# Applying an RMS norm's factor to the results of the projections instead of to their input, in a fused three-layer kernel

## The chip, the cores and the metric

The kernel runs on one core of a Trainium2 chip. The metric is the device time of one launch in microseconds (us). Matrix products run on TensorE (PE in the profile; its weight loads are PEld), elementwise work on VectorE (DVE) and ScalarE (ACT); SyncE (SP) starts the loads of the weights.

## The reference

Three layers work on x, 256 tokens by 1024 features, in f32. The first two have this form (their feed-forward part is left out below, and so is the third layer, which the change does not touch):

```
h = rmsnorm(x, norm_mix[l])            # x * rsqrt(mean(x*x) + eps) * g
proj = h @ w_in[l]
aq, ak, av, iq, ik, iw, hq, hf, hi, hg, ga, gb = jnp.split(proj, split_points, axis=-1)
y_attn = dsa_attention(rope(norm(aq)), rope(norm(ak)), av, iq, ik, iw)   # top 64 keys per query
f = lb + (1 - lb) * sigmoid(hf)        # forget factor; the key is (1 - lb) * sigmoid(-hf)
o = recurrence(silu(hq), 1 - f, hi, f)
y_hgrn = rmsnorm(o) * silu(hg)
merged = sigmoid(ga) * (y_attn @ w_proj_attn[l]) + sigmoid(gb) * (y_hgrn @ w_proj_hgrn[l])
x = x + merged @ w_out[l]
```

The norm's factor, rsqrt(mean(x*x) + eps), is one number per token. So (x * factor * g) @ w equals factor * ((x * g) @ w).

## The kernel before

All weights come from HBM once, in units of 1 MB (half of that for some): `UNITS` lists them in the order in which PE uses them. A unit is loaded into one of six `raw` buffers. Then it is split into two parts of the type f32r: ACT writes `w_hi` (a rounded copy, `split` in the block of ScalarE, shown as L953), DVE writes `w_lo` (what is left, L1425). There are three buffers of each, so the split of unit m waits for the end of unit m-3 on PE. The activations are split in the same way, and each product is three matmuls: hi with hi, lo with hi, and hi with lo (`three`, L508 to L510).

Each of PE, ACT and DVE has its own stream of instructions in a fixed order, written out by hand, and passes it from the front. Semaphores tie the streams together. On ACT and DVE a call of `tick()` steps to the next unit and issues the split of the unit three ahead of it. `unit_in()` waits for PE to end a unit, `emptied()` frees its PSUM bank. There are four banks called `stream` for the units and four called `steps` for the rest.

In a mixer (the part of a layer ahead of its feed-forward part) the units are, in order: ix0, ix1 (index queries and keys), aq0, aq1, ak0, ak1, av0, av1 (attention), hf0, hf1 (forget), hq0, hq1, hg0, hg1 (recurrence), ga0, ga1 (gate), hi0, hi1, ga2, ga3, gb0 to gb3. Those with two banks (ix, aq, ak, av, hi) have tokens on the partitions; the others have features on the partitions, and their result is 128x512 for a unit, the two halves of the features side by side.

The norm is used in two ways. Up to ak1, PE multiplies the input times the norm's weights only (`x_gained_hi`, `x_gained_lo`), since the factor isn't known yet; ACT applies the factor when it empties the banks, as the scale of its copy. From av0 on PE multiplies the normalised input (`h_hi`, `h_lo`). `normalise` (L1492) makes it: DVE multiplies x, weight and factor into `h_norm` (8 instructions, L1506), ACT rounds it into `h_hi` (`normed_hi`, 4), DVE subtracts into `h_lo` (4, L1501).

Around the first of the two blocks of 128 queries, the streams are these. PE: hf1, then the first logits (L696), then hq0, then the transposes of the probabilities (L704), then hq1. DVE: the mask and the row maximum of each head from the logits (L1617, L1621), one split, the second half of the selection of keys for the second query block (`next(chosen[1])`, L1595 to L1604), two splits, then the keys and forget factors (L1798 to L1801), which wait for hf1. ACT: sigmoids of hf0 and hf1 straight from their banks (`scratch` and `hgrn_k_in_order`, L1206 and L1207), then the exponentials of the first block, one per head (`probs`, L1052), which wait for the row maximum.

```
1787  first, second = attend(b, 0, sel[:, 0, 0:P]), attend(b, 1, sel[:, 1, :])
1788  dve.wait_ge(*s_sel.at(b, 0))
1789  next(first)
1790  tick()
1791  next(chosen[1])
1792  tick(2)
1793
1794  dve.wait_ge(*evacuated(unit(b, "hf1")))
```

The second query block follows in the same way: logits after hg1, the transposes after ga0. ACT's exponentials of it come after its Silu of hg1.

Of the kernel before, what the change touches and what calls it, by code (L numbers as in the profile page):

```python
# [131 lines left out]
def scaled_after(u):  # L132
    return u[1] < 2 and (u[2] in ("ix0", "ix1", "aq0", "aq1", "ak0", "ak1") or u[0] in ("gate", "up") and u[2] < 2)
# [10 lines left out]
def evac_engine(u):  # L144
# [4 lines left out]
    if kind == "merge" or (kind == "out" and b < 2) or (kind == "gate" and scaled_after(u)) or name in ("val0", "val1", "f") or shifted(u):  # L149
        return "dve"  # L150
# [35 lines left out]
def build(nc, a, out):  # L186
# [26 lines left out]
    flip = at("reversed_ident", [P, P], F32, 155)  # L213
    v_back = at("v_reversed", [P, 512], F32, 173)
# [181 lines left out]
    g_sig = Event("gates_set", 2)  # L396
# [106 lines left out]
    def _(pe):  # L503
# [33 lines left out]
        def stream(count, before=None, between=None):  # L537

            for _ in range(count):
# [15 lines left out]
                h_h, h_l = (xg_h, xg_l) if scaled_after(UNITS[m]) else (xs_h, xs_l) if shifted(UNITS[m]) else (hh, hl)  # L555
# [109 lines left out]
        def normed(ni, pairs=range(4)):  # L665
            return {2 * j: [n_lo.at(ni, j)] for j in pairs}
# [119 lines left out]
        def mixer(b):  # L786
# [30 lines left out]
            stream(1, normed(ni, (0, 1)))  # L817
            stream(1, normed(ni, (2, 3)))
            stream(1)
# [24 lines left out]
            pe.wait_ge(*evacuated(unit(b, "hq1")))  # L844
# [98 lines left out]
    def _(act):  # L943
# [33 lines left out]
        def here():  # L977
            return cur[0] - 1
# [32 lines left out]
        def gained_hi(ni, g, j):  # L1011

            dst = xg_h if ni < 4 else xs_h[:, :, 0:T]
# [7 lines left out]
        def normed_hi(ni):  # L1021
            for j in range(4):
                act.wait_ge(*n_hn.at(ni, j))
# [95 lines left out]
        def mixer(b, x_ready):  # L1119
# [34 lines left out]
            for j in range(2):  # L1154
# [4 lines left out]
                else:  # L1159
# [3 lines left out]
                    normed_hi(2 * b)  # L1163
# [5 lines left out]
            act.wait_ge(*n_lo.upto(2 * b))  # L1169
# [28 lines left out]
            for j in range(2):  # L1198
                tick()
                unit_in()  # L1200
# [10 lines left out]
            unit_in()  # L1211
            f(hq[:, 0:2, :], b2(here()), ACT.Silu).then_inc(*emptied())
            next(first)
            tick()
            unit_in()
            f(hq[:, 2:4, :], b2(here()), ACT.Silu).then_inc(*emptied())
            tick()
            unit_in()
            f(hg[:, 0:2, :], b2(here()), ACT.Silu).then_inc(*emptied())
            next(first)  # L1220
            tick()
# [191 lines left out]
    def _(dve):  # L1413
# [328 lines left out]
        def mixer(b):  # L1742
# [80 lines left out]
            for i in range(7):  # L1823
# [6 lines left out]
                if i % 2:  # L1830
                    tick()
# [309 lines left out]
```

## Time and profile before

| what | value |
|---|---|
| median of 3 runs | 1191.14 us (1190.63 to 1192.18) |
| the profiled execution, its own time | 1191.75 us |
| its span in the trace | 1190.0 us |
| busy PE, DVE, ACT | 1138.2, 858.1, 631.4 us |
| mean granted clock of PE, as a share of full speed | 0.992 |

The profile shows one execution. The span runs from the first to the last instruction in the trace, and the time measured for the same execution is 1.75 us more. Times inside the trace count from the start of the span. In the trace the first mixer stands between about 11 and 230 us, the second between about 431 and 643 us. An instruction's row gives its start and its length; a group's row gives its total and mean, and in brackets how long its engine stood idle before it and what ended that.

### The profile page before, as it was taken

How to read it: one execution, taken by the hardware profiler on the slowest of the kernel's cores; microseconds unless marked ns; L12 is line 12 of the kernel's file. 1: busy time of each engine (PE TensorE's matmuls, PEld its weight loads, DVE VectorE, ACT ScalarE, POOL GpSimd, SP SyncE). 2: the span in 40 equal slices, each digit the busy share in tenths (PEclk: the TensorE clock that was granted, in tenths of full speed). 3: DMA queues.
4: the chain of work that ended last, by engine and by line, in shares of the span. 5: the costliest groups of instructions: out<-in, count | busy, mean ns of one | idle time of the engine just before them, and what ended most of it. 6: DMA issues, size and time to landing. Idle time of an engine off the chain costs nothing.

```text
span 1190.0 us, 20981 instructions
## 1 busy us (share of the span) xinstructions
PE 1138.2 (96%) x8858; PEld 1102.4 (93%) x8858; DVE 858.1 (72%) x1376; ACT 631.4 (53%) x790; POOL 0.2 (0%) x4
## 2 busy tenths in 40 slices
PE   5999999999999999999999999999999989999996
PEld 5789899999999998998999999999989879999996
DVE  6996566777988879956667778887899756554443
ACT  7676366464443456764655544444687555433333
POOL 0000000000000000000000000000000000000000
PEclk9999999999999999999999999999999999999998
DMA  9555433756879554464437488795443333655511
GB/s 347 155 175 177 142 116 133 235 191 225 278 251 318 173 171 152 144 186 131 142 128 254 150 270 277 250 305 161 136 161 123 106 106 107 208 182 177 177 36 36
DMA packets 177613, 214.14 MB, mean 180 GB/s; under 512 B 3696, under 2 KB 160752, under 8 KB 177520
## 3 DMA queue, kind: packets, MB, share of 16 engines
q1 hardware_dynamic: 176800, 211.86, 54.5%
q8 instruction: 70, 1.15, 0.4%
q10 hardware_dynamic: 720, 0.94, 0.2%
q14 instruction: 23, 0.19, 0.1%
HBM read 211.74 MB, written 1.05 MB: 179 GB/s over the span
## 4 chain that ended last, share of the span: by engine, by line
PE 72%; DVE 18%; ACT 7%; issue 2%; DMA 1%; SPq 0%; DVEq 0%; ACTq 0%
PE stream L508 16%; PE stream L510 16%; PE stream L509 16%; DVE w_lo L1425 7%; PE steps L508 5%; PE steps L510 5%; PE steps L509 5%; ACT w_hi L953 3%; PE steps L714 1%; PE stream L735 1%; PE steps L864 1%; DVE conv_acc L1995 1%; DVE h_norm L1506 1%; DVE score L1597 1%; ACT probs L953 1%
## 5 line engine op out<-in xcount | busy, mean ns | idle before, releaser
L1425 DVE TENSOR_TENSOR w_lo<-raw,w_hi 128x2048 fp32r<-128x2048 f32 (+2 forms) x178 | 401.2, 2265 | 207.2 <-ACT w_hi L953 206.6
L953 ACT ACTIVATE w_hi<-raw 128x2048 fp32r<-128x2048 f32 (+2 forms) x178 | 336.3, 1893 | 287.9 <-PE stream L510 256.9
L508 PE MATMUL stream<-h_hi,w_hi 128*128 128x256 f32 x1576 | 451.2, 286 | 8.4 <-DVE w_lo L1425 7.4
L509 PE MATMUL stream<-h_lo,w_hi 128*128 128x256 f32 x1576 | 445.8, 283 | 0.0
L510 PE MATMUL stream<-h_hi,w_lo 128*128 128x256 f32 x1576 | 445.8, 283 | 0.0
L508 PEld LDWEIGHTS stream<-h_hi,w_hi 128*128 128x128 f32 x1576 | 302.2, 192 | 13.1 <-DVE w_lo L1425 10.8
L509 PEld LDWEIGHTS stream<-h_lo,w_hi 128*128 128x128 f32 x1576 | 302.4, 192 | 1.0 <-issue 1.0
L510 PEld LDWEIGHTS stream<-h_hi,w_lo 128*128 128x128 f32 x1576 | 302.2, 192 | 0.0
L508 PE MATMUL steps<-gu_hi,w_hi 128*128 128x256 f32 x528 | 149.8, 284 | 1.5 <-DVE gu_lo L1727 1.5
L509 PE MATMUL steps<-gu_lo,w_hi 128*128 128x256 f32 x528 | 149.4, 283 | 0.0
L510 PE MATMUL steps<-gu_hi,w_lo 128*128 128x256 f32 x528 | 149.4, 283 | 0.0
L508 PEld LDWEIGHTS steps<-gu_hi,w_hi 128*128 128x128 f32 x528 | 101.3, 192 | 2.1 <-issue 1.8
L509 PEld LDWEIGHTS steps<-gu_lo,w_hi 128*128 128x128 f32 x528 | 101.3, 192 | 0.0
L510 PEld LDWEIGHTS steps<-gu_hi,w_lo 128*128 128x128 f32 x528 | 101.3, 192 | 0.0
L1681 DVE SCALAR_TENSOR_TENSOR ada_sum<-ada_raw,c_act,ada_sum 128x256 f32<-128x256 f32 x168 | 81.5, 485 | 6.0
L953 ACT ACTIVATE gu_hi<-gu 128x512 fp32r<-128x512 f32 x33 | 20.8, 632 | 102.8 <-DVE gu L1723 98.7
L581 PE MATMUL stream<-w_hi,x_gained_hi 128*128 128x512 f32 (+1 forms) x96 | 37.3, 388 | 11.4 <-DVE w_lo L1425 11.4
L1995 DVE SCALAR_TENSOR_TENSOR conv_acc<-conv_in,params,conv_acc 128x256 f32<-128x256 f32 x90 | 38.9, 480 | 1.0
L1727 DVE TENSOR_TENSOR gu_lo<-gu,gu_hi 128x512 fp32r<-128x512 f32 x33 | 22.9, 693 | 23.0 <-ACT gu_hi L953 23.0
L508 PE MATMUL stream<-x_gained_hi,w_hi 128*128 128x256 f32 x128 | 36.8, 287 | 1.0 <-DVE x_gained_lo L1479 1.0
L509 PE MATMUL stream<-x_gained_lo,w_hi 128*128 128x256 f32 x128 | 36.2, 283 | 0.0
L510 PE MATMUL stream<-x_gained_hi,w_lo 128*128 128x256 f32 x128 | 36.2, 283 | 0.0
(307 smaller groups left out, 1634.9 us busy)
## 6 DMA issues: line engine op xcount, KB each, us to landing
raw<-in_w_ffn_in SPq DMA_DIRECT2D x66, 1024.0 KB, 5.5
raw<-in_w_in SPq DMA_DIRECT2D x54, 1024.0 KB, 5.4
raw<-in_w_ffn_out SPq DMA_DIRECT2D x33, 1024.0 KB, 5.3
ada_raw<-in_ada_w SPq DMA_DIRECT2D x24, 1024.0 KB, 6.6
raw<-in_w_out SPq DMA_DIRECT2D x8, 1024.0 KB, 5.1
raw<-in_w_proj_attn SPq DMA_DIRECT2D x8, 512.0 KB, 3.5
raw<-in_w_proj_hgrn SPq DMA_DIRECT2D x8, 512.0 KB, 4.6
raw<-in_w_o SPq DMA_DIRECT2D x4, 1024.0 KB, 5.2
```

Source lines behind the costliest of these rows:

```text
L508: pe.matmul(dst, w_h, x_h, start=start, stop=False, skip_group_check=True)
L509: pe.matmul(dst, w_h, x_l, start=False, stop=False, skip_group_check=True)
L510: return pe.matmul(dst, w_l, x_h, start=False, stop=stop, skip_group_check=True)
L581: pe.matmul(dst, h_h[:, k0 + k, ts], hi[:, k, :], start=k0 + k == 0, stop=False)
L714: mm = pe.matmul(pv[:, DH * h:DH * h + DH], prT[:, h, s, :], v[:, s, DH * h:DH * h + DH], start=s == 0, stop=s == qt)
L735: mm = pe.matmul(conv_bank[:, 0:T], diag[j], upad[:, 3, j:j + T], start=j == 0, stop=j == CONV_K - 1)
L864: mm = pe.matmul(level_bank(i)[:, c, :], kp[i % 2][:, c, :], qp[:, c, :].rearrange("p (n two h) -> p n two h", two=2, h=h)[:, :, 1, :], st ...
L953: return act.activation(out_, in_, func, **kw)
L1425: tt(wl[m % SPL][:, 0:n], raw[m % RAW][:, 0:n], wh[m % SPL][:, 0:n].bitcast(F32), ALU.subtract)\
L1681: ins = stt(acc, w[:, k, :], cact[:, k:k + 1], acc, ALU.mult, ALU.add)
L1727: tt(gu_l[i % 2].rearrange("p c t -> p (c t)"), gu, gu_h[i % 2].rearrange("p c t -> p (c t)").bitcast(F32), ALU.subtract).then_inc(*lane.m ...
L1995: ins = stt(cv[:, c, :], src, w, cv[:, c, :], ALU.mult, ALU.add)
```

## The change

In the first two layers PE multiplies the input times the norm's weights in every unit of the mixer. It is now held in `h_hi` and `h_lo` (ACT and DVE write it there where they wrote `x_gained`), and `normalise` is not called for these mixers. The factor is applied to results:

- hf, hq, hg, ga0, ga1, gb2 and gb3 (10 units per mixer) are emptied by DVE, which multiplies the bank by the factor (`scaled_evac`, into `scratch`, `hgrn_q`, `hgrn_gate`, `gate_a`, `gate_b`). The sigmoids and Silus of ACT then read these tiles and wait for DVE.
- ga2, ga3, gb0 and gb1 are still copied by ACT, and DVE multiplies them in place later, four features' chunks at a time.
- av and hi get the factor as a scale of ACT's copy.
- The factor is copied to `rstd_kept`, since `gate_b` covers the tile `rstd`.

The diff, cut to its core:

```diff
 def scaled_after(u):
-    return u[1] < 2 and (u[2] in ("ix0", "ix1", "aq0", "aq1", "ak0", "ak1") or u[0] in ("gate", "up") and u[2] < 2)
+    return u[1] < 2 and (u[0] in ("tw", "fm") or u[0] in ("gate", "up") and u[2] < 2)
+def scaled_by_dve(u):
+    return u[1] < 2 and u[2] in ("hf0", "hf1", "hq0", "hq1", "hg0", "hg1", "ga0", "ga1", "gb2", "gb3")
...
# TensorE, mixer
-            stream(1, normed(ni, (0, 1)))
-            stream(1, normed(ni, (2, 3)))
-            stream(1)
+            stream(3)
...
# ScalarE, mixer
-                    normed_hi(2 * b)
...
-            act.wait_ge(*n_lo.upto(2 * b))
...
-                unit_in()
                 for i in range(2 * (1 - j)):
                     act.wait_ge(*qk_t.at(b, 2 + i))
...
-                act.wait_ge(*s_used.at(b, 1))
-                f(scr[:, 2 * j:2 * j + 2, :], b2(here()), ACT.Sigmoid).then_inc(*lane.step())
-                f(hkn[:, 2 * j:2 * j + 2, :], b2(here()), ACT.Sigmoid, scale=-1.0).then_inc(*emptied())
+                act.wait_ge(*evacuated(here()))
+                z = scr[:, 2 * j:2 * j + 2, :]
+                f(hkn[:, 2 * j:2 * j + 2, :], z, ACT.Sigmoid, scale=-1.0).then_inc(*lane.step())
+                act.wait_ge(*lane.last)
+                f(z, z, ACT.Sigmoid).then_inc(*lane.mark(f_act))
             first, second = attend(b, 0), attend(b, 1)
+            def activated(x, event):
+                tick()
+                act.wait_ge(*evacuated(here()))
+                f(x, x, ACT.Silu).then_inc(*lane.mark(event))
             next(first)
+            activated(hq[:, 0:2, :], q_act)
+            next(first)
+            activated(hq[:, 2:4, :], q_act)
+            activated(hg[:, 0:2, :], hg_act)
+            next(first)
+            activated(hg[:, 2:4, :], hg_act)
+            next(second)
...
# VectorE, mixer
-            normalise(2 * b, lambda k: pc("norm_mix", 8 * b + k))
...
+            def scaled_tick(dst):
+                step()
+                scaled_evac(dst)
+                split_ahead()
             next(first)
-            tick()
+            scaled_tick(scr[:, 0:2, :])
             next(chosen[1])
-            tick(2)
-            dve.wait_ge(*evacuated(unit(b, "hf1")))
+            scaled_tick(scr[:, 2:4, :])
+            scaled_tick(hq[:, 0:2, :])
+            dve.wait_ge(*f_act.at(b, 1))
...
+            dve.tensor_copy(rs_kept, rs).then_inc(*lane.step())
+            scaled_tick(hq[:, 2:4, :])
             next(first)
-            tick()
+            scaled_tick(hg[:, 0:2, :])
             next(first)
             dve.wait_ge(*s_sel.at(b, 1))
             next(second)
-            tick(3)
+            scaled_tick(hg[:, 2:4, :])
+            scaled_tick(ga[:, 0:2, :])
+            scaled_tick(ga[:, 2:4, :])
             next(second)
...
+            wide_rs = rs_kept.unsqueeze(1).broadcast_to([P, 4, T])
+            dve.wait_ge(*evacuated(unit(b, "ga3")))
+            tt(ga[:, 4:8, :], ga[:, 4:8, :], wide_rs, ALU.mult).then_inc(*lane.mark(g_scaled))
             tick()
-            tick()
+            dve.wait_ge(*evacuated(unit(b, "gb1")))
+            tt(gb[:, 0:4, :], gb[:, 0:4, :], wide_rs, ALU.mult).then_inc(*lane.mark(g_scaled))
+            scaled_tick(gb[:, 4:6, :])
...
-            tick()
+            step()
+            scaled_evac(gb[:, 6:8, :], rs_kept)
+            split_ahead()
```

How the instructions stand, first on VectorE in the first mixer, from the row maximum of the first query block to the split after the selection of keys (rows that repeat are left out). Before:

```order
L1621 SCALAR_TENSOR_TENSOR row_max<-row_max,qk_sumsq 128x8
L1425 TENSOR_TENSOR w_lo_60<-raw_54,w_hi_57 128x2048
L1595 MAX top_188<-score 128x8
L1597 MATCH_REPLACE score<-top_188,score 128x256
...
L1602 TENSOR_SCALAR sel_bias<-score 128x256
L1604 SCALAR_TENSOR_TENSOR sel_bias<-sel_bias,consts 128x256
L1425 TENSOR_TENSOR w_lo_58<-raw_49,w_hi_55 128x2048
```

Now (the two reads of `stream` are hf0 and hf1):

```order
L1620 SCALAR_TENSOR_TENSOR row_max<-row_max,qk_sumsq 128x8
L1488 TENSOR_TENSOR scratch<-stream,rstd 128x512
L1424 TENSOR_TENSOR w_lo_60<-raw_54,w_hi_57 128x2048
L1594 MAX top_189<-score 128x8
L1596 MATCH_REPLACE score<-top_189,score 128x256
...
L1601 TENSOR_SCALAR sel_bias<-score 128x256
L1603 SCALAR_TENSOR_TENSOR sel_bias<-sel_bias,consts 128x256
L1488 TENSOR_TENSOR scratch<-stream,rstd 128x512
L1424 TENSOR_TENSOR w_lo_58<-raw_49,w_hi_55 128x2048
L1488 TENSOR_TENSOR hgrn_q<-stream,rstd 128x512
```

Hf0 is emptied behind the row maximum, hf1 behind the selection. On ScalarE at the same place, from the copies of the keys to the exponentials of the first query block, the order of instructions is the same, but the inputs are others. Before:

```order
L953 ACTIVATE kT<-steps 128x512 x2
L953 ACT_TABLE_LOAD
L953 ACTIVATE scratch<-stream 128x512
L953 ACTIVATE hgrn_k_in_order<-stream 128x512
L953 ACTIVATE w_hi_55<-raw_49 128x2048
L953 ACTIVATE scratch<-stream 128x512
L953 ACTIVATE hgrn_k_in_order<-stream 128x512
L953 ACT_TABLE_LOAD
L953 ACTIVATE probs,row_sum<-probs,row_max,qk_sumsq 128x128 x8
```

Now:

```order
L960 ACTIVATE kT<-steps 128x512 x2
L960 ACT_TABLE_LOAD
L960 ACTIVATE hgrn_k_in_order<-scratch 128x512
L960 ACTIVATE scratch<-scratch 128x512
L960 ACTIVATE w_hi_55<-raw_49 128x2048
L960 ACTIVATE hgrn_k_in_order<-scratch 128x512
L960 ACTIVATE scratch<-scratch 128x512
L960 ACT_TABLE_LOAD
L960 ACTIVATE probs,row_sum<-probs,row_max,qk_sumsq 128x128 x8
```

The sigmoids ahead of `probs` now read what DVE has written to `scratch`. The third place is VectorE at the second query block, from its row maximum on (hg1, ga0 and ga1). Now:

```order
L1620 SCALAR_TENSOR_TENSOR row_max<-row_max,qk_sumsq 128x8
L1488 TENSOR_TENSOR hgrn_gate<-stream,rstd 128x512
L1424 TENSOR_TENSOR w_lo_59<-raw_53,w_hi_56 128x2048
L1488 TENSOR_TENSOR gate_a<-stream,rstd 128x512
L1424 TENSOR_TENSOR w_lo_60<-raw_54,w_hi_57 128x2048
```

Before, the three splits stood there alone; the multiplications of `hgrn_gate` and `gate_a` are new.

## Rows read from the trace of the kernel before

**Rows 1.** The page: busy us, share of the span, instructions of each engine.

```profile
PE 1138.2 (96%) x8858; PEld 1102.4 (93%) x8858; DVE 858.1 (72%) x1376; ACT 631.4 (53%) x790; POOL 0.2 (0%) x4
```

**Rows 2.** PE's waits from 0 to 215 us: us in total, times, longest us.

```profile
PE stream L508 <- DVE w_lo L1425: 2.3, 2, 1.2
PE steps L675 <- DVE q_tm L1566: 1.3, 1, 1.3
...
PE steps L675 <- DVE k_tm L1574: 0.2, 1, 0.2
```

**Rows 3.** PE's waits from 430 to 630 us, the second mixer.

```profile
PE stream L508 <- DVE w_lo L1425: 1.9, 2, 1.2
```

**Rows 4.** PE's waits over the whole span.

```profile
PE steps L887 <- ACT scratch L953: 0.8, 2, 0.4
```

**Rows 5.** A stretch: length, busy PE, PEld, DVE, ACT, POOL, granted clock, DMA.

```profile
60.00:70.00 10.00, 9.76 (x67) 8.79 (x67) 9.72 (x14) 5.92 (x8) 0.00 (x0) 1.00 0.61 194
```

**Rows 6.** Groups by line and shape: count, busy us, mean ns, idle before.

```profile
L1506 DVE SCALAR_TENSOR_TENSOR h_norm<-xT,params,rstd 128x256 f32<-128x256 f32 x32 | 13.7, 479 | 0.0
L1501 DVE TENSOR_TENSOR h_lo<-h_norm,h_hi 128x512 fp32r<-128x512 f32 x16 | 11.0, 687 | 0.7 <-ACT h_hi L953 0.3
L1489 DVE TENSOR_TENSOR silu_g<-stream,rstd 128x512 f32<-128x512 f32 x4 | 2.7, 684 | 0.0
L953 ACT ACTIVATE silu_g<-silu_g 128x512 f32<-128x512 f32 x4 | 2.5, 632 | 5.9 <-DVE silu_g L1489 5.9
```

**Rows 7.** Instructions of DVE, first query block, first mixer: start us, us.

```profile
80.15 0.28 DVE L1617 CUSTOM_DVE_ANT_0 probs<-steps,sel_bias 128x128 f32<-128x128 f32 x1
...
81.96 0.17 DVE L1621 SCALAR_TENSOR_TENSOR row_max<-row_max,qk_sumsq 128x8 f32<-128x8 f32 x1
82.04 2.29 DVE L1425 TENSOR_TENSOR w_lo<-raw,w_hi 128x2048 fp32r<-128x2048 f32 x1
84.25 0.42 DVE L1595 MAX8 top<-score 128x8 f32<-128x256 f32 x1
...
88.84 2.29 DVE L1425 TENSOR_TENSOR w_lo<-raw,w_hi 128x2048 fp32r<-128x2048 f32 x1
```

**Rows 8.** Instructions of ACT, the same place.

```profile
80.27 0.59 ACT L953 ACTIVATE hgrn_k_in_order<-stream 128x512 f32<-128x512 f32 x1
80.88 1.28 ACT L953 ACT_TABLE_LOAD   x1
82.17 0.50 ACT L953 ACTIVATE probs<-probs,row_max,qk_sumsq 128x128 f32<-128x128 f32 x1
...
85.93 0.19 ACT L953 ACTIVATION_READ_ACCUMULATOR probs<-probs,row_max,qk_sumsq 128x1 f32 x1
```

**Rows 9.** Instructions of PE, the same place: logits, hq0's first, transposes.

```profile
77.81 1.26 PE L696 MATMUL steps<-kT,qT 64*128 64x128 f32 x16
80.29 0.39 PE L508 MATMUL stream<-h_hi,w_hi 128*128 128x256 f32 x1 [1.22 <-DVE w_lo L1425]
...
86.17 0.55 PE L704 MATMUL steps<-consts,probs 128*128 128x128 f32 x3
```

**Rows 10.** ACT, second mixer: the square of the attention queries.

```profile
456.98 1.06 ACT L953 ACTIVATE qk_square<-q_tm 128x1024 f32<-128x1024 f32 x1
```

**Rows 11.** DVE, second mixer: its next step, which reads that square.

```profile
459.04 1.21 DVE L1563 TENSOR_REDUCE qk_sumsq<-qk_square 128x16 f32<-128x1024 f32 x1
```

**Rows 12.** Second query block, first mixer, ACT and PE.

```profile
111.06 0.60 ACT L953 ACTIVATE probs<-probs,row_max,qk_sumsq 128x256 f32<-128x256 f32 x1 [0.52 <-DVE row_max L1621]
...
115.91 1.31 PE L704 MATMUL steps<-consts,probs 128*128 128x128 f32 x10 [1.18 <-ACT probs L953]
```

**Rows 13.** Stretches at PE's wait in the third layer (columns as in 5).

```profile
974.00:979.37 5.37, 0.00 (x0) 0.03 (x1) 4.13 (x10) 3.33 (x9) 0.00 (x0) 0.72 0.40 159
979.37:983.30 3.93, 3.93 (x17) 3.72 (x17) 3.83 (x9) 1.96 (x5) 0.00 (x0) 0.52 0.00 0
983.30:985.59 2.29, 2.29 (x18) 2.19 (x17) 1.67 (x4) 2.26 (x4) 0.00 (x0) 1.00 0.04 11
```

More of the change, by code:

```diff
@@ L148, in evac_engine @@
         return "gu"
-    if kind == "merge" or (kind == "out" and b < 2) or (kind == "gate" and scaled_after(u)) or name in ("val0", "val1", "f") or shifted(u):
+    if scaled_by_dve(u) or kind == "merge" or (kind == "out" and b < 2) or (kind == "gate" and scaled_after(u)) or name in ("val0", "val1", "f") or shifted(u):
         return "dve"
@@ L554, in stream @@
                 before = None
-                h_h, h_l = (xg_h, xg_l) if scaled_after(UNITS[m]) else (xs_h, xs_l) if shifted(UNITS[m]) else (hh, hl)
+                h_h, h_l = (xg_h, xg_l) if scaled_after(UNITS[m]) and kind in ("gate", "up") else (xs_h, xs_l) if shifted(UNITS[m]) else (hh, hl)
                 def in_order(n_out, n_in):
@@ L665, in normed @@
         def normed(ni, pairs=range(4)):
-            return {2 * j: [n_lo.at(ni, j)] for j in pairs}
+            return {2 * j: [n_lo.at(NTH_NORM[ni], j)] for j in pairs}
         def gained(ni, pairs=range(4)):
@@ L843, in mixer @@
             pe.wait_ge(*r_k.at(b))
-            pe.wait_ge(*evacuated(unit(b, "hq1")))
+            pe.wait_ge(*q_act.at(b, 1))
             pe.wait_ge(*a_lo.at(b, 1))
@@ L1204, in mixer @@
                         .then_inc(*lane.mark(qkT_set))
[L1205 to L1207 removed]
+                act.wait_ge(*evacuated(here()))
[3 more added lines that the diff above has]
+                f(z, z, ACT.Sigmoid).then_inc(*lane.mark(f_act))
             first, second = attend(b, 0), attend(b, 1)
+            def activated(x, event):
+                tick()
+                act.wait_ge(*evacuated(here()))
+                f(x, x, ACT.Silu).then_inc(*lane.mark(event))
             next(first)
+            activated(hq[:, 0:2, :], q_act)
[5 more added lines that the diff above has]
+            next(second)
             tick()
[L1211 to L1213 removed]
+            next(second)
             tick()
[L1215 to L1233 removed]
             def pack(i):
@@ L1248, in mixer @@
             wide_evac(v)
-            gates = [ga[:, 2 * j:2 * j + 2, :] for j in (2, 3)] + [gb[:, 2 * j:2 * j + 2, :] for j in range(4)]
+            gates = [ga[:, 2 * j:2 * j + 2, :] for j in (2, 3)] + [gb[:, 2 * j:2 * j + 2, :] for j in range(2)]
             def copied(i, rows, t, n):
@@ L1282, in mixer @@
                     f(AT[:, :, 2, :], level_bank(i), ACT.Copy).then_inc(*lane.mark(r_copy))
-            act.wait_ge(*evacuated(unit(b, "ga3")))
+            act.wait_ge(*g_scaled.at(b, 0))
             f(ga, ga, ACT.Sigmoid).then_inc(*lane.mark(g_sig))
-            evac_copy(gates.pop(0))
+            tick()
             for i in range(2):
@@ L1807, in mixer @@
             next(second)
-            tick(3)
+            scaled_tick(hg[:, 2:4, :])
+            scaled_tick(ga[:, 0:2, :])
+            scaled_tick(ga[:, 2:4, :])
             next(second)
             tick()
-            dve.wait_ge(*evacuated(unit(b, "hq1")))
+            dve.wait_ge(*q_act.at(b, 1))
             for g in range(2):
```

36 lines of the change are left out of this document (14 added, 22 removed).

## The prediction

> **What bounds the kernel now.** I read the page's busy times first: PE is busy 1138.2 us of a span of 1190.0 [rows 1]. The change leaves PE's matmuls as they are. So the time can move only by PE's waits, and by the clock at which PE runs behind them. The table of PE's waits comes next. In the first mixer, 2.3 us go to splits that DVE delivered late, and 1.3 and 0.2 us to rotated queries and keys, also from DVE [rows 2]; in the second mixer, 1.9 us go to splits [rows 3]. These are the waits in which normalising can have a part: DVE is busy 9.72 us of 10 in such a stretch, while the clock is at its full level [rows 5]. Last I read where each engine stands around the first query block [rows 7 to 9], since the order of instructions shows that the change puts DVE between PE and ACT there.
>
> **What is taken away.** Per mixer DVE loses 8 multiplications at 0.48 us and 4 subtractions at 0.69 [rows 6]. Their sum is 6.6 us; as neighbours overlap by some 0.07 us, 5.8 remain. ACT loses four copies. DVE, which is full there, comes that much earlier to the late splits and rotations. In the first mixer all three kinds of wait are shorter than 5.8 us and go: -3.8 us. In the second, DVE's lead is smaller. Its first reduction of queries starts at 459.04 [rows 11] and needs ACT's square, done at 456.98 + 1.06 = 458.04 [rows 10]: at least 1.0 us of lead. The square itself comes earlier by at most the four copies that go, 4 x 0.63 = 2.5 us [rows 6]; most of these ran while ACT would have waited for PE. So the lead is 1.0 to 3.5 us, and I take 1.8, nearer to the end that has a row; that is about enough for both late splits: -1.9 us. PE's wait for the squares of the recurrence's output, 0.8 us over both mixers [rows 4], goes too, since ACT no longer copies gb2 ahead of them. Together -6.5 us.
>
> **What comes in at the first query block.** On ACT the exponentials stand behind the sigmoids of hf1, as before, but these now read what DVE has emptied, and DVE empties hf1 behind the selection of keys. From the end of the row maximum (82.13) the chain is now:
>
> - DVE empties hf0, 0.6 us (0.68 less the overlap) [rows 6], and makes its split, 84.25 - 82.04 = 2.2 us [rows 7];
> - the second half of the selection, 88.84 - 84.25 = 4.6 us [rows 7], and hf1 emptied, 0.7: so far 8.0 us from the row maximum, as the first step starts 0.1 before its end;
> - ACT's two sigmoids at 0.63 us [rows 6], the table load for the exponential, 1.3 us, which was hidden before, and the exponentials, 82.17 to 86.12, or 4.0 us with the passing on [rows 8].
>
> That makes 14.6 us, where it was 4.0. PE meanwhile has only hq0 to do, 86.17 - 80.29 = 5.9 us [rows 9]. The row maximum ended 82.13 - 79.07 = 3.1 us behind the logits; the masks and maxima alone take 2.0 us (80.15 to 82.13) and can start when the first pair of logits is out, some 0.8 us before the last (1.26 us for four pairs [rows 9], and a little to pass it on). So it ends 1.2 us behind them at best. In the first mixer, where DVE has its full lead, I take this: PE waits 1.2 + 14.6 - 5.9 = 9.9 us. In the second, the logits come 0.7 us earlier and DVE 1.8 us: the masks then start 1.1 - 1.1 = 0 us behind the logits, and PE waits 2.0 + 14.6 - 5.9 = 10.7 us. Sum +20.6 us; with 1.0 and 3.1 us at the ends, 19.4 to 23.6.
>
> What queues behind: PE's values, its later units and every split behind hq0 slide by the same amount, so that this wait isn't met again. The splits for hq1 and hg0 are ready before PE resumes.
>
> **The second query block.** DVE empties hg1 only behind the row maximum of this block, and ACT's Silu of hg1 stands ahead of its exponentials. Before, these started at once behind the row maximum (111.06, after a wait of 0.52), and PE waited 1.18 us [rows 12]. Now 0.6 us for the emptying, 0.63 for the Silu and 1.28 for the table load, which can't start before, come in between: +2.5 us, twice, +5.1.
>
> **The clock.** The wait of 5.37 us in the third layer shows what a long idle does. The mean granted clock over it is 0.72, then 0.52 for 3.93 us of matmuls, the level of 1.2 GHz. The same pieces of work take 2.29 us when it is back at 1.00 [rows 13]. That is 1.6 us lost, and each wait of 10 us must lose it too: +3.3 us. The second waits will be 3.7 us long, between 1.18 us, where nothing shows, and 5.37; so between 0 and 1.6 us each. They lie nearly in the middle, and I take 0.8: +1.6. The Trainium skill (TensorE: Matmul & The Clock Gate, HAM oscillation — how this bites in real kernels) says that an idle PE falls back to half clock and that half of the time spent there is lost; by that the 3.93 us would cost 2.0 instead of 1.6 us, and the sum would be 0.7 us higher.
>
> **The rest costs nothing.** Of the other emptyings, hq0 falls into DVE's time before PE resumes; hq1, hg0, ga0, ga1 come just behind the end of their unit, where DVE has to wait for ACT's half of the next split anyway. If that cover is gone, a split is 0.6 us later, and two units are still split ahead. The multiplications of ga2 to gb1, two of 128x1024, fall into idle time of DVE behind the recurrence; of gb2 and gb3 one replaces a copy of ACT. The scales on ACT's copies add little, on an engine with room (5.92 us of 10 [rows 5]). No queue of SP is touched; loads follow the splits.
>
> **Sum.** -6.5 + 20.6 + 5.1 + 3.3 + 1.6 = 24.1 us. The profiled execution took 1191.75 us (span 1190.0), 0.6 above the median of 1191.14, so I put the same sum on the median: 1215.2 us.
>
> **The rivals.**
> 1. *The clock costs nothing.* PE resumes with transposes and is soon level again. Against it speaks [rows 13]. It would give 24.1 - 4.9 = 19.2 us: 1210.3. Chance 0.10.
> 2. *A change of table costs more than its load.* Four loads that were hidden stand on the path. The trace shows no more than the load: it starts 0.02 us behind the sigmoid's end (80.27 + 0.59), and the exponential starts 0.01 us behind the load's end [rows 8]. A further 1.4 us at each of the four would give 1220.7 us. The Trainium skill (ScalarE: Activation LUTs, What ACT_TABLE_LOAD costs) gives 2.66 us for a switch, 1.38 of them a drain beside the load; the trace doesn't agree. Chance 0.05.
> 3. *DVE is the bound and the hold is short.* If the sigmoids of hf1 found DVE's result early, only DVE's added work would count: 10 emptyings at 0.6, two wide products of 1.2 each and a copy make 8.6 us against 5.8 taken away, +2.8 per mixer, or 5.6, with the second block's 5.1 and nothing gained: 1201.8. Against it: the order of instructions has the selection ahead of hf1. Chance 0.10.
> 4. *Faster: the hold is hidden.* The 6.5 us of waits go, and the exponentials still reach PE within its stream of hq0. Row maximum at 1.2 us and 4.0 us of exponentials leave 0.7 us of room against 5.9. The hold must then be under 0.7 us instead of 10.6, and the second block hidden too: 1184.6. With 5.1 us paid there, the kernel breaks even where the first hold is 1.4 us. Chance 0.04.
>
> That the change doesn't do what it says is ruled out by the order of the instructions, but an unforeseen cancellation stays: 0.02 for no change.
>
> **The numbers.** Forecast 0.69, rivals 0.10, 0.05, 0.10, 0.04, no change 0.02. Predicted 1215.2. The range holds forecast and rivals 1 and 2. Its low end takes no clock loss and the shortest waits (1210.3 - 1.2 = 1209.1), its high end the longest waits of the first block (+3.0) and 1.6 us for each clock loss (+1.6), 1219.8, and rival 2: 1208 to 1221. A measurement of this kernel can tell 0.2% or 2.4 us from no change. Slower by more 0.94, within 0.02, faster 0.04.
>
> **What would show it.** In the profile after: a wait of PE for `probs` of 9 to 12 us in each mixer, and one of 3 to 4 us, where each had 1.2; DVE's emptying of hf1 directly behind the selection; ACT's first exponential 9 to 11 us behind the row maximum; a granted clock near 0.5 behind the long waits; no wait for `q_tm` or `k_tm` and hardly one for `w_lo` in the mixers. I am wrong if PE's waits for `probs` sum to less than 15 us, or if the time falls.

## The result, and the profile after

The changed kernel is slower: 1223.57 us, the median of four runs (1222.69 to 1224.76), against 1191.46 us for the kernel before in four runs. The ratio is 1.027, with a 95% interval of 1.0255 to 1.0286. The profiled execution took 1223.65 us, with a span of 1221.5 us and a mean granted clock of 0.980. Against the profiled execution of before that is 31.9 us more, 31.5 of it in the span. The forecast was 1215.2 us with a range from 1208 to 1221: the direction was right and so were the places that it named, but one place was missing, and the time lies 2.6 us above the range.

The page of the profile after, busy times [rows 1] and clock:

```profile
PE 1144.9 (94%) x8858; PEld 1110.2 (91%) x8858; DVE 865.4 (71%) x1378; ACT 624.6 (51%) x774; POOL 0.2 (0%) x4
...
PEclk9999999999999999989999999999999998999998
```

PE has the same 8858 matmuls and is busy 6.7 us longer; its mean granted clock is 0.980, where it was 0.992. DVE gained 7.3 us, ACT lost 6.8; neither is near its limit. PE's waits over the whole span, after (us in total, times, longest):

```profile
PE steps L713 <- ACT probs L960: 28.3, 4, 10.4
PE stream L517 <- DVE gate_b L1488: 4.2, 2, 2.1
PE stream L517 <- DVE w_lo L1424: 4.2, 6, 1.2
```

The first row is the forecast one: four waits for `probs` in the mixers. The second was not forecast. No wait for `q_tm`, `k_tm` or the squares is left [rows 2, 4].

The first query block on DVE, which answers to [rows 7] (start us, us, engine, line, instruction, idle before it):

```profile
76.85 0.17 DVE L1620 SCALAR_TENSOR_TENSOR row_max<-row_max,qk_sumsq 128x8 f32<-128x8 f32 x1
76.93 0.68 DVE L1488 TENSOR_TENSOR scratch<-stream,rstd 128x512 f32<-128x512 f32 x1
77.53 2.28 DVE L1424 TENSOR_TENSOR w_lo<-raw,w_hi 128x2048 fp32r<-128x2048 f32 x1
...
83.99 0.43 DVE L1603 SCALAR_TENSOR_TENSOR sel_bias<-sel_bias,consts 128x256 f32<-128x256 f32 x1
84.33 0.68 DVE L1488 TENSOR_TENSOR scratch<-stream,rstd 128x512 f32<-128x512 f32 x1
```

The same place on ACT, as in [rows 8]:

```profile
78.32 0.63 ACT L960 ACTIVATE scratch<-scratch 128x512 f32<-128x512 f32 x1
78.86 1.90 ACT L960 ACTIVATE w_hi<-raw 128x2048 fp32r<-128x2048 f32 x1
85.05 0.63 ACT L960 ACTIVATE hgrn_k_in_order<-scratch 128x512 f32<-128x512 f32 x1 [4.29 <-DVE scratch L1488]
85.71 0.63 ACT L960 ACTIVATE scratch<-scratch 128x512 f32<-128x512 f32 x1
86.36 1.28 ACT L960 ACT_TABLE_LOAD   x1
87.66 0.49 ACT L960 ACTIVATE probs<-probs,row_max,qk_sumsq 128x128 f32<-128x128 f32 x1
```

And on PE, as in [rows 9]:

```profile
73.42 1.26 PE L705 MATMUL steps<-kT,qT 64*128 64x128 f32 x16
75.19 0.39 PE L517 MATMUL stream<-h_hi,w_hi 128*128 128x256 f32 x1 [0.50 <-DVE w_lo L1424]
...
91.63 1.97 PE L713 MATMUL steps<-consts,probs 128*128 128x128 f32 x8 [10.43 <-ACT probs L960]
```

One reads the hold from top to bottom: the row maximum ends at 77.02, hf0 is emptied, a split is made, the selection runs to its end, and only then hf1 is emptied (84.33). ACT stood idle 4.29 us for that. From the row maximum to PE's first transpose it is 91.63 - 77.02 = 14.6 us, to the tenth the number of the forecast.

What the trace says of the term that was missed, PE first, then DVE, at the start of the first mixer's merge units:

```profile
203.23 0.28 PE L519 MATMUL stream<-ya_hi,w_lo 128*128 128x256 f32 x1
205.60 0.36 PE L517 MATMUL stream<-ya_hi,w_hi 128*128 128x256 f32 x1 [2.09 <-DVE gate_b L1488]
...
206.15 0.42 PE L517 MATMUL stream<-ya_hi,w_hi 128*128 128x256 f32 x1
206.36 0.41 PE L518 MATMUL stream<-ya_lo,w_hi 128*128 128x256 f32 x1
```

```profile
198.58 1.23 DVE L1853 TENSOR_TENSOR scratch<-scratch,hgrn_gate 128x1024 f32<-128x1024 f32 x1
203.62 1.23 DVE L1855 TENSOR_TENSOR yh_lo<-scratch,yh_hi 128x1024 fp32r<-128x1024 f32 x1 [3.82 <-ACT yh_hi L960]
204.77 0.68 DVE L1488 TENSOR_TENSOR gate_b<-stream,rstd_kept 128x512 f32<-128x512 f32 x1
```

The second merge unit writes to the bank that holds gb3. Before, ACT copied gb3 out of it ahead of `yh_hi`, and PE came for the bank 0.2 us after the end of that copy. The rows of the kernel before, ACT, then PE:

```profile
191.26 0.57 ACT L953 ACTIVATE gate_b<-stream 128x512 f32<-128x512 f32 x1
191.73 1.05 ACT L953 ACTIVATE yh_hi<-scratch 128x1024 fp32r<-128x1024 f32 x1
...
192.06 0.28 PE L508 MATMUL stream<-ya_hi,w_hi 128*128 128x256 f32 x1
```

Now the step is DVE's and stands behind `yh_lo`, behind a wait of 3.82 us, so PE stops for 2.09 us. The matmuls behind that stop follow each other at 0.21 us (206.15 to 206.36); those ahead of it at 0.12. The granted clock was 1.00 over the stop and 0.50 from 206.15 to 209.10.

**The ledger.** Since PE's instructions are the same and in the same order, its loss can be read off as the shift of each piece of work. Starts on PE, us:

| piece of PE's work | before | after | shift | change of the shift |
|---|---|---|---|---|
| hq0, first mixer | 80.29 | 75.19 | -5.10 | -5.10 |
| transposes, first block | 86.17 | 91.63 | +5.46 | +10.56 wait |
| values, first block | 92.86 | 100.56 | +7.70 | +2.24 clock |
| transposes, second block | 115.91 | 126.14 | +10.23 | +2.53 wait |
| values, second block | 123.47 | 135.25 | +11.78 | +1.55 clock |
| squares of the recurrence | 181.61 | 192.90 | +11.29 | -0.49 |
| squares for the next norm | 242.10 | 257.19 | +15.09 | +3.80 gb3 |
| hq0, second mixer | 493.20 | 506.36 | +13.16 | -1.93 |
| transposes, first block | 499.07 | 522.81 | +23.74 | +10.58 wait |
| values, first block | 505.76 | 531.28 | +25.52 | +1.78 clock |
| transposes, second block | 528.80 | 556.86 | +28.06 | +2.54 wait |
| values, second block | 536.37 | 566.03 | +29.66 | +1.60 clock |
| squares of the recurrence | 594.51 | 623.68 | +29.17 | -0.49 |
| squares for the next norm | 655.00 | 686.47 | +31.47 | +2.30 gb3 |
| end of PE's work | 1179.86 | 1211.38 | +31.52 | +0.05 |

Sums: -8.0 gone, +26.2 in waits for the exponentials, +7.2 of clock behind them, +6.1 at gb3 (4.6 of wait in both mixers and 1.5 of clock in the first). The same reading is used for every experiment below. It compares single executions, and up to hq0 it carries some chance: ten profiles (the changed kernel's and those of its variants below) run the same instructions up to there, and hq0 starts in them between 75.13 and 76.38 us. The clock's share was read from stretches around the first wait (columns as in [rows 5]):

```profile
81.20:91.63 10.43, 0.00 (x1) 0.00 (x0) 6.41 (x13) 6.52 (x20) 0.00 (x0) 0.75 0.60 195
91.63:95.60 3.97, 3.97 (x19) 3.97 (x20) 2.19 (x1) 3.94 (x4) 0.00 (x0) 0.50 0.03 10
95.60:99.60 4.00, 4.00 (x31) 4.00 (x31) 2.80 (x8) 0.69 (x2) 0.00 (x0) 0.87 0.69 206
```

### The profile page after: what moved, and what is told of

It is laid out like the page before. It is cut to its first block, busy times and chain, and to the rows that moved or that the text cites. A ratio compares the mean times of both kernels' runs of the same rounds, so it can differ in the third digit from the quotient of the medians.

```text
span 1221.5 us, 20961 instructions
## 1 busy us (share of the span) xinstructions
PE 1144.9 (94%) x8858; PEld 1110.2 (91%) x8858; DVE 865.4 (71%) x1378; ACT 624.6 (51%) x774; POOL 0.2 (0%) x4
## 4 chain that ended last, share of the span: by engine, by line
PE 72%; DVE 16%; ACT 7%; issue 2%; DMA 1%; SPq 0%; DVEq 0%; ACTq 0%
PE stream L517 15%; PE stream L518 15%; PE stream L519 15%; DVE w_lo L1424 6%; PE steps L517 5%; PE steps L519 5%; PE steps L518 5%; ACT w_hi L960 3%; ACT probs L960 1%; PE steps L723 1%; DVE score L1596 1%; PE stream L744 1%; PE steps L871 1%; DMA raw<-in_w_in 1%; PE steps L713 1%
## 5 line engine op out<-in xcount | busy, mean ns | idle before, releaser
L590 PE MATMUL stream<-w_hi,h_hi 128*128 128x512 f32 (+1 forms) x160 | 62.2, 388 | 12.1 <-DVE w_lo L1424 12.1
L592 PE MATMUL stream<-w_lo,h_hi 128*128 128x512 f32 (+1 forms) x160 | 60.5, 378 | 0.0
L591 PE MATMUL stream<-w_hi,h_lo 128*128 128x512 f32 (+1 forms) x160 | 60.4, 378 | 0.0
L590 PEld LDWEIGHTS stream<-w_hi,h_hi 128*128 128x128 f32 x160 | 30.7, 192 | 17.7 <-issue 12.1
```

Source lines behind the costliest of these rows:

```text
L590: pe.matmul(dst, h_h[:, k0 + k, ts], hi[:, k, :], start=k0 + k == 0, stop=False)
L591: pe.matmul(dst, h_l[:, k0 + k, ts], hi[:, k, :], start=False, stop=False)
L592: mm = pe.matmul(dst, h_h[:, k0 + k, ts], lo[:, k, :], start=False, stop=k0 + k == KC - 1)
```

## The experiments

**Theory A**: everything lost is PE's waiting for three results that stand late in their engine's order (hf1 behind the selection, hg1's Silu ahead of the second exponentials, gb3 behind `yh_lo`), and the lower clock behind these waits. Taking away the normalised input is itself worth 8 us. **The rivals**: the waits come from DVE's added work; gb3's wait only covers another; the low clock has nothing to do with the waiting; the change lost time in a further place. The kernel before ran beside each group of experiments, with medians of 1191.87 us (1 to 4), 1191.77 (5 to 8), 1191.35 (9, 10) and 1191.57 (11); "less" below is against the changed kernel's 1223.57.

### 1. gb3 emptied ahead of the wait

```diff
             tt(scr, scr, hg, ALU.mult).then_inc(*lane.mark(r_y))
+            step()
+            scaled_evac(gb[:, 6:8, :], rs_kept)
             dve.wait_ge(*r_hi.at(b))
             tt(yh_l, scr, yh_h.bitcast(F32), ALU.subtract).then_inc(*lane.mark(r_lo))
-            step()
-            scaled_evac(gb[:, 6:8, :], rs_kept)
             split_ahead()
```

> The changed kernel (1223.6 us) with one step of VectorE moved: it empties gb3 before it waits for the rounded yh, not behind yh_lo. Theory A (TensorE's 2.1-us wait for gb3's bank, ahead of the second merge unit of each mixer, is time of the kernel): both waits go, 4.2 us, and with the first mixer's wait the low granted clock behind it, up to 1.5 us: 1218 to 1219.5. Theory B (the wait only takes the place of one that comes next, for yh_lo or for the gates' sigmoids): under 1 us is won, 1222.6 to 1223.6, and a new wait of about 2 us stands at the same place under another name.

Measured: 1216.63 us, 6.9 less than the changed kernel and 1.4 below A's range. PE's wait for `gate_b` is gone and no other has come; DVE has the step within its old idle time:

```profile
201.11 0.69 DVE L1488 TENSOR_TENSOR gate_b<-stream,rstd_kept 128x512 f32<-128x512 f32 x1 [0.86 <-PE stream L519]
```

In the ledger the two pieces up to the next norm's squares shrink by 3.79 and 2.29 us, the 3.80 and 2.30 of the table. The other 0.8 us is in places that the edit doesn't touch: this profile reached hq0 1.06 us later, lost 0.72 and 0.30 us less of clock behind the first blocks' waits, and 0.99 us less behind the mixers, where it didn't have a fall of the clock that the changed kernel's trace shows near 936 us. Theory A.

### 2. The first block's exponentials between hf0 and hf1

```diff
             for j in range(2):
                 tick()
...
+                if j:
+                    first, second = attend(b, 0), attend(b, 1)
+                    next(first)
                 act.wait_ge(*evacuated(here()))
                 z = scr[:, 2 * j:2 * j + 2, :]
...
-            first, second = attend(b, 0), attend(b, 1)
...
-            next(first)
             activated(hq[:, 0:2, :], q_act)
```

> The changed kernel with one thing of ScalarE moved: the eight exponentials of the first query block stand between hf0's and hf1's sigmoids, so they no longer wait for VectorE's selection. Theory A (the 10.4-us wait is the hold by hf1, which VectorE empties only behind the selection): row maxima end at 77.0, hf0's two sigmoids by about 79, table load 1.3 and exponentials 3.8 end at about 84; TensorE is free at 81.2, so a wait of 3 us stays of 10.4. Two mixers: 15 us less, and some 2 to 4 us less of low clock behind: 1204.5 to 1207. Theory B (the wait is mostly the exponentials' own time and the late row maxima): 3 to 5 us less in all, 1218 to 1220.

Measured: 1214.4 us (1210.89 to 1215.41), 9.2 less, between the two ranges and in neither. The wait of 10.4 us fell to 4.85, not to 3.0:

```profile
79.31 1.90 ACT L960 ACTIVATE w_hi<-raw 128x2048 fp32r<-128x2048 f32 x1
81.22 1.28 ACT L960 ACT_TABLE_LOAD   x1
82.52 0.49 ACT L960 ACTIVATE probs<-probs,row_max,qk_sumsq 128x128 f32<-128x128 f32 x1
```

My expectation had left out the split that goes with hf1's step, 1.90 us on ACT ahead of the table load; this and 4.85 - 1.90 = 2.95 us make up the forecast wait. The ledger shows -5.6 us at the transposes of each mixer, and back +0.8 and +0.7 us behind the two waits of the second mixer and +1.5 at its gb3, where the clock now fell too. So the hold is what theory A says, and B's 3 to 5 us are too little; but the gain from a shorter wait is partly given back by where the clock falls next.

### 3. The second block's exponentials ahead of hg1's Silu

```diff
-            activated(hg[:, 2:4, :], hg_act)
             next(second)
+            activated(hg[:, 2:4, :], hg_act)
```

> The changed kernel with ScalarE's exponentials of the second query block ahead of hg1's Silu. Theory A: TensorE's second wait falls from 3.7 to about 1.2 us as before the change, two mixers 5.0 us; and as the granted clock behind a wait of 1.2 us stayed whole in the kernel before, up to 3 us more: 1215.5 to 1218.6. Theory B (hg1's Silu is then late for VectorE's y, and the wait comes back in the gated part): 1221 or more.

Measured: 1217.2 us, 6.4 less. Both waits fell by 2.54 us, to 1.17, and with each the slower stretch behind it, 1.55 and 1.61 us. Against these 8.2 us, the second mixer's gb3 cost 1.5 more than in the changed kernel's trace, since the clock fell there, and the stretches behind the first blocks' waits cost 0.4 and 0.5 more. Theory A, with the price of each wait confirmed.

### 4. PE kept at work while it waits

```diff
             yield
+            if b < 2:
+                pe.wait_ge(*a_mx.at(b, qt))
+                for _ in range(24 if qt else 72):
+                    pe.matmul(A[3][:, 0:T], hh[:, 0, 0:P], hh[:, 1, :], start=True, stop=True)
             pe.wait_ge(*a_ex.at(b, qt))
```

> The changed kernel with TensorE kept at work in its two waits for exponentials: 72 matmuls of 128x256 (9 us at 0.125 us each) in the first wait and 24 (3 us) in the second, into a bank that nobody reads, so that the waits keep their ends. Their results are used by nobody. Theory A (some 7 of the 32 us are a lower granted clock behind waits): no wait ends later, the transposes take 1.1 us (not 2.0) and 2.0 (not 2.6), and the time falls by 5 to 8 us, to 1215.5 to 1218.6. Theory B (the low clock is that of the transposes and of what surrounds them, not of the idle time): within 1 us of 1223.6.

Measured: 1219.63 us (1214.92 to 1220.58), 3.9 less: the direction of A, but 1.0 short of its range. The wait of the first block ends at 91.59, where it ended at 91.63, and none of the others ends later against what stands ahead of it. Three stretches: the second mixer from the end of the added matmuls on, first block and second block; and, last, what follows the wait of the first mixer's first block:

```profile
518.75:522.75 4.00, 2.18 (x20) 2.18 (x20) 0.40 (x1) 3.98 (x10) 0.00 (x0) 1.00 0.53 183
552.00:555.86 3.86, 3.01 (x28) 3.01 (x28) 1.23 (x1) 3.86 (x8) 0.00 (x0) 1.00 0.22 75
...
91.59:95.50 3.91, 3.91 (x20) 3.91 (x21) 2.13 (x1) 3.88 (x4) 0.00 (x0) 0.56 0.05 14
```

In three of four places the clock stayed whole, and the ledger shows -1.79, -1.55 and -1.61 us there: all of the 1.78, 1.55 and 1.60 of the table. In the first mixer's first block the remaining idle time of 1.82 us was enough for a fall (0.56 over the next 3.9 us), and 0.7 of 2.24 came back; at the second mixer's gb3, 1.5 us were lost that the changed kernel's trace doesn't have. In the profiles without the added matmuls the clock fell at each of the six stops of 10.4 us (the changed kernel, experiments 1 and 3) and each of the eight of 3.7 us (the changed kernel, experiments 1, 2 and 5), so three of four without a fall is hardly chance: the idle time is what lowers the clock. My 5 to 8 us had counted on all four places and on nothing given back.

### 5. The selection behind hf1

```diff
-            next(chosen[1])
             scaled_tick(scr[:, 2:4, :])
+            next(chosen[1])
             scaled_tick(hq[:, 0:2, :])
```

> The changed kernel with VectorE's emptying of hf1 (and the split behind it) ahead of the rest of the selection, ScalarE's order untouched. Theory A (the hold is the chain selection, emptying, sigmoids, table load, exponentials): hf1 is empty at about 80.9, ScalarE's next split of w_hi ends at 81.2, sigmoids 82.5, load 83.8, exponentials 87.6; TensorE free at 81.2 waits 6.4 instead of 10.4: 8 us less in all, 1214.5 to 1216.5. Theory B (any late order costs the same, since TensorE's wait is set by the selection itself): within 2 us of 1223.6.

Measured: 1216.43 us, 7.1 less; the waits are 6.0 instead of 10.4, the ledger shows -4.4 us at each, and again 1.5 us back at the second mixer's gb3. Theory A: of the 4.6 us of selection that no longer stand ahead of hf1, PE's wait gives back 4.4.

### 6 and 7. The waits alone, in the kernel before

Nothing of the change is in these two: the input is normalised and ACT empties its banks as before. The first adds

```diff
                 act.wait_ge(*s_used.at(b, 1))
+                if j:
+                    act.wait_ge(*s_sel.at(b, 1))
                 f(scr[:, 2 * j:2 * j + 2, :], b2(here()), ACT.Sigmoid).then_inc(*lane.step())
```

> The kernel before (1191.9 us) with one wait added: ScalarE's sigmoids of hf1 wait until VectorE has finished the selection of the second query block, which is where the change makes them wait. Nothing else changes. Theory A (the hold alone makes the long waits): the selection ends at 88.9, two sigmoids 1.2, table load 1.3, exponentials 3.9: TensorE, free at 86.3, starts at 95.3, 9.0 us of wait in each mixer, and 1.8 to 2.2 us of low clock behind each: 18.0 + 4.0, so 1213.9 (1212 to 1216). Theory B (the long waits need VectorE's added multiplications): under 5 us are added, 1192 to 1197.

and the second adds to it

```diff
+            act.wait_ge(*a_mx.at(b, 1))
             f(hg[:, 2:4, :], b2(here()), ACT.Silu).then_inc(*emptied())
...
-            evac_copy(gates.pop(0))
+            tick()
             act.wait_ge(*r_y.at(b))
             f(yh_h, scr, ACT.Copy).then_inc(*lane.mark(r_hi))
+            act.wait_ge(*r_lo.at(b))
+            unit_in()
+            f(gates.pop(0), b2(here()), ACT.Copy).then_inc(*emptied())
```

> The kernel before with three waits added and nothing else: hf1's sigmoids behind the selection, hg1's Silu behind the row maxima of the second query block, and ScalarE's copy of gb3 behind yh_lo. Theory A (these three are the whole loss, and what the change takes away is worth 8 us): 1213.9 of the first, then the second waits of some 3.0 us for 1.2 (3.6 in all) with about 3 of clock, and two waits of about 2 us for gb3's bank (4) with 0 to 3.4 of clock: 1226.5 (1223 to 1230), above the changed kernel. Theory B (the change lost time in another place too, so that the waits alone give less): below 1221.

Measured: 1213.63 us (+21.9) and 1224.54 us (+32.8; ratio 1.0278, interval 1.0262 to 1.0293), both within A's ranges. PE's waits in the second:

```profile
PE steps L704 <- ACT probs L953: 24.5, 4, 9.1
...
PE stream L508 <- ACT gate_b L953: 4.2, 2, 2.1
```

Its ledger: 18.5 us at the first blocks, 3.9 at the second, 6.2 of clock behind them, and 2.34 and 2.35 at gb3, where this time the clock did not fall: 33.2 us in all with the small changes. So three waits in an otherwise untouched kernel make most of the changed kernel's loss, which is 39.5 us before the 8.0 gained are taken off. From here the changed kernel differs by -7.8 (normalising gone), +2.6 and +1.1 (DVE's emptyings as further links of the two holds), +1.0 of clock behind them and +1.4 at gb3 (the clock). That is -1.7 us, the difference of the two spans (1221.48 against 1223.13); the medians differ by 1.0. That the two kernels take nearly the same time is thus a cancellation, not a proof; the proof is that each piece is accounted for, and nothing is left for a further place.

### 8. All three holds away

```diff
             for j in range(2):
                 tick()
...
+                if j == 0:
+                    first, second = attend(b, 0), attend(b, 1)
+                    next(first)
```

with the moves of 1 and 3.

> The changed kernel with all three holds taken away: ScalarE's exponentials of the first query block directly behind the row maxima, ahead of all four sigmoids of hf0 and hf1; those of the second ahead of hg1's Silu; VectorE empties gb3 ahead of its wait for the rounded yh. Theory A (the changed kernel is the kernel before, less 8.0 us, plus waits and the clock behind them): exponentials start at 77.5 with no table load ahead and end at 81.4, TensorE is free at 81.2; all of 21.1 + 5.1 + 4.2 of waits and 9.1 of clock go: 1223.6 - 39.5 = 1184.1 (1183 to 1186). Theory B (the sigmoids, now late, hold hgrn_k, gates or the next mixer step, or the low clock comes at other places too): 1188 or more.

Measured: 1197.39 us, 0.5% above the kernel before: neither A's 1184 nor, in its reason, B quite. No wait is left at the transposes of the first block or at gb3. But PE stops one step later:

```profile
81.34 1.28 ACT L960 ACT_TABLE_LOAD   x1
82.63 0.63 ACT L960 ACTIVATE hgrn_k_in_order<-scratch 128x512 f32<-128x512 f32 x1
...
86.83 1.90 ACT L960 ACTIVATE w_hi<-raw 128x2048 fp32r<-128x2048 f32 x1
88.74 1.28 ACT L960 ACT_TABLE_LOAD   x1
90.03 0.63 ACT L960 ACTIVATE hgrn_q<-hgrn_q 128x512 f32<-128x512 f32 x1
90.57 1.06 ACT L960 ACTIVATE probsT<-steps 128x512 f32<-128x512 f32 x2
```

```profile
91.29 1.48 PE L723 MATMUL steps<-v,probsT 128*128 128x64 f32 x10 [3.08 <-ACT probsT L960]
```

The four sigmoids, two splits, two table loads and a Silu, 9.2 us of ACT's queue (81.34 to 90.57), now stand between the exponentials and the copies of the turned probabilities. Against the kernel before this costs 6.3 and 6.4 us per mixer (3.2 of wait, 3.1 and 3.2 of clock behind it); all the rest is -7.2.

### 9 and 10. Two ways past the next wait

Both start from the version of 8. The first also moves DVE's hf1 ahead of the selection (as in 5) and hq0's Silu behind the copies; the second leaves DVE alone and puts the copies ahead of hf1's sigmoids:

```diff
                 if j == 0:
                     first, second = attend(b, 0), attend(b, 1)
                     next(first)
+                else:
+                    next(first)
```

> The version of the run before with two more moves, since there the wait went from the exponentials to ScalarE's copies of the turned probabilities, which stood behind hf1's sigmoids: VectorE empties hf1 ahead of the rest of the selection, and ScalarE's copies of the first query block stand ahead of hq0's Silu. Theory A (each wait there is ScalarE's order alone): copies at about 89 for a need at 88.5; all of the new waits and the clock behind them go: 1184 (1183 to 1187), 7 to 8 us faster than the kernel before. Theory B (ScalarE has too much work between the row maxima and the copies, whatever its order): a wait of 1 to 3 us at the copies in each mixer, 1188 to 1194.

> The same aim in another way: VectorE's order is that of the changed kernel but for gb3 (hf1 emptied behind the selection), and ScalarE's exponentials and copies of the first query block both stand ahead of hf1's sigmoids, those of the second block ahead of hg1's Silu. Theory A (nothing of TensorE's needs hf1 early): copies are done when the bank is turned, no wait at either, 1184 (1183 to 1187). Theory B (hf1's sigmoids at 88 or later hold VectorE's forget gates and so y_tm, or hq1's Silu): a wait for y_tm or hgrn_k of 1 to 3 us in each mixer, 1187 to 1194.

Measured: 1201.21 us and 1191.74 us (eleven runs; ratio to the kernel before 1.0003, interval 0.9994 to 1.0011). Both miss A. The first lies above B's range too: the waits at the copies that B named are there, but only 1.1 us each, and the larger ones, 3.25 and 4.73 us, are for `y_tm`, which neither theory had. The second lies in B's range, with B's reason. In the first, DVE reaches the split that goes with hf1 before ACT has made its half of it, and stands still for 5 us with the selection queued behind:

```profile
86.12 2.29 DVE L1428 TENSOR_TENSOR w_lo<-raw,w_hi 128x2048 fp32r<-128x2048 f32 x1 [5.02 <-ACT w_hi L960]
...
101.46 0.69 DVE L1633 TENSOR_TENSOR y_tm<-steps,row_sum 128x512 f32<-128x512 f32 x1
```

In the second, DVE makes its forget gates and `hgrn_k` (2.5 us, 91.73 to 94.23) ahead of `y_tm`, with the emptying of hq1 and a split behind them; PE needs `y_tm` at 95.56:

```profile
91.73 1.38 DVE L1804 TENSOR_SCALAR scratch<-scratch,one_minus_lb,lower_bound 128x256 f32<-128x256 f32 x4
...
97.46 0.69 DVE L1631 TENSOR_TENSOR y_tm<-steps,row_sum 128x512 f32<-128x512 f32 x1
```

```profile
98.21 0.61 PE L730 MATMUL steps<-consts,y_tm 128*128 128x128 f32 x2 [2.65 <-DVE y_tm L1631]
```

### 11. y_tm ahead of the forget gates

```diff
-            dve.wait_ge(*f_act.at(b, 1))
...
             scaled_tick(hq[:, 2:4, :])
             next(first)
+            dve.wait_ge(*f_act.at(b, 1))
...
             scaled_tick(hg[:, 0:2, :])
```

The lines left out are the forget gates and both halves of `hgrn_k`, which move with the wait; `rs_kept` stays where it was.

> The version of the run before (ScalarE's exponentials and copies ahead of hf1's sigmoids), which ran as fast as the kernel before, with one more move on VectorE: the forget gates and hgrn_k (4.4 us of work) stand behind y_tm and no longer ahead of it. Theory A (the 2.65-us wait for y_tm in each mixer, and 1.6 us of low clock behind the first, are all that is left of the loss): 1191.7 - 5.3 - 1.6 = 1184.8 (1183.5 to 1186.5), faster than both kernels. Theory B (the late forget gates, or hg0's later emptying, are waited for instead): 1188 or more.

Measured: 1186.44 us (1186.13 to 1187.07), ratio to the kernel before 0.9959, interval 0.9945 to 0.9973: faster than both, and within A's range. The expectation called the moved work 4.4 us; it is 2.5. The wait for `y_tm` is 0.9 us in each mixer, not gone (DVE still makes two splits ahead of it, and in the first mixer stands still for 0.65 us for ACT's half of one), and the clock is whole behind it. PE's waits and the page's busy times:

```profile
PE steps L713 <- ACT probs L960: 2.3, 2, 1.2
...
PE steps L730 <- DVE y_tm L1631: 1.8, 2, 0.9
```

```profile
PE 1135.7 (96%) x8858; PEld 1101.3 (93%) x8858; DVE 865.2 (73%) x1378; ACT 624.4 (53%) x774; POOL 0.2 (0%) x4
```

DVE and ACT do the work of the changed kernel to within 0.2 us, and PE is 37 us of span ahead of it. This rules out DVE's added work as the cause.

## Why the prediction was wrong, and where right

- **What is taken away**, forecast -6.5, measured -8.0: -5.1 in the first mixer (forecast -3.8), -1.9 in the second (-1.9), -1.0 at the squares (-0.8). The mechanism was right. In the first mixer the three kinds of wait that I counted went, except 0.5 us for hq0's split, which stayed: 3.3 us. The other 1.8 us are spread over many small steps, the largest 0.4 us; how much of them DVE's lead brought isn't shown. With the latest of the ten starts of hq0 (76.38 us) the -5.1 would have been -3.9.
- **The first query block**, forecast 9.9 + 10.7 = 20.6, measured 10.56 + 10.58 = 21.1. Chain and length were right. The row maximum ended 77.02 - 74.68 = 2.3 us behind the logits, where I had put 1.2 as the best case; hq0's wait of 0.5 us took back part of that.
- **The second query block**, forecast +5.1, measured 2.53 + 2.54 = 5.1.
- **The clock**, forecast 3.3 + 1.6 = 4.9, measured 7.2 behind these four waits. The 1.6 us of [rows 13] is the price of one wait of 5.4 us; behind 10.4 us it was 2.24 and 1.78, and behind 3.7 us it was already the full 1.55 and 1.60, where I took 0.8 as the middle of an interval. A row inside it was in the trace of before and I didn't look: in the third layer PE stops for 1.39 us, until 902.9, and the granted clock is 0.51 from 904.60 to 908.00. Taking the upper bound for both would have given 6.5. The Trainium skill (TensorE: Matmul & The Clock Gate, HAM oscillation — how this bites in real kernels) puts the penalty at half the time spent at the lower clock. By that the estimate for the stretches shown above is 3.97 x 0.5 + 4.00 x 0.13 = 2.5 us, against 2.24 in the ledger: the trace about agrees.
- **The step that failed** is "The rest costs nothing", in its words "of gb2 and gb3 one replaces a copy of ACT". As a count it is off by one, for before, ACT copied both (at 180.49 and 191.26), and the count is the wrong question: I named what the step costs DVE, and not who waits for the bank that it empties nor what it now stands behind. It cost 4.6 us of wait and 1.5 of clock, 6.1 of the 7.4 us that were missing. Experiment 1 shows it alone: gb3's step moved, those 6.1 us came back.
- **The sum**: 24.1 forecast; 31.5 = 24.1 + 6.1 (gb3) + 2.3 (clock) + 0.5 (first block) - 1.5 (more taken away). Against the measured median the forecast is short by 8.4 us, 1.0 more than that: the time outside the span grew by 0.4, and I had put the sum on a median that lay 0.6 below the profiled execution. The range failed since none of its terms allowed for a wait in a place that I had priced at nothing.
- **The rivals.** The clock is not free (experiment 4 rules out rival 1). DVE is not the bound (rival 3; experiment 11). The hold was not hidden (rival 4), though with other orders it can be: 1186.44 us against the 1184.6 worked out for it. A table switch costs its load (rival 2): ACT's load at 86.36 lasts 1.28 us and the exponential starts at 87.66, 0.02 us later. The Trainium skill (ScalarE: Activation LUTs, What ACT_TABLE_LOAD costs) has 2.66 us for a switch; the trace doesn't agree.
- Of what was named as signs, the waits for `probs` (28.3 us), hf1 behind the selection, the first exponential 10.6 us behind the row maximum and the clock of 0.50 all showed; `q_tm` and `k_tm` are gone.

## What to carry to other kernels

When emptying a bank moves from one engine to another, ask three things of each bank: what the step now stands behind, who comes for the bank next, and how long before that it used to be free; the cost of the instruction itself is the least of it. For gb3 the old margin was 192.06 - 191.83 = 0.2 us. A wait that is removed shows the next one in the same engine's order (exponentials, copies, `y_tm`), so follow the whole chain of the block before moving one step; and price every new stop of TensorE with its clock.

## What was not expected of the hardware

- A stop of 3.7 us cost as much clock as one of 5.4 (1.55 and 1.60 us against 1.6). Behind each stop of 3.1 us or more in a mixer the granted clock was at half for some microseconds, in every profile here; behind the second blocks' stops of 1.2 us (two in the kernel before, two in experiment 3) it stayed whole. That is no rule for short stops: behind the 1.1-us stop for the copies in experiment 9 the clock fell in the first mixer (0.60 from 92.70 to 96.00) and not in the second, and behind the 1.39-us stop in the third layer it fell in 8 of the 13 profiles.
- Between these the same stop sometimes lowers the clock and sometimes not. Behind the 2.1-us stop for gb3 it fell in 9 of 12 cases (six profiles of two mixers each), at 1.5 us each; behind 2.65 us in experiment 10 in the first mixer, not in the second; behind 1.82 us in experiment 4 likewise. Experiments 2 to 5 each lost 1.5 us at the second mixer's gb3 in this way, where the changed kernel's own trace lost none. What decides it, no run here shows; executions of one and the same kernel differ in their clock too (experiment 4: 1214.92 us at a mean clock of 0.992, 1220.58 at 0.988). A single profile is therefore no measure of such a stop's price, and 1.5 us more or less there can't be put down to an edit.
- At the lower clock the 128x256 matmuls follow each other at 0.21 us instead of 0.12, and the eight transposes of a first block take 1.97 us instead of 1.09.
